# Residual merge and three later norms by halves of the tokens, with late modulation and softmax scaling moved

## The reference

```python
# layer 1
mod = silu(c) @ w_ada + b_ada                 # 6 vectors of 1024: sh1, sc1, g1, sh2, sc2, g2
h = rmsnorm(x) * (1 + sc1) + sh1
q, k, v, u_pool = split(h @ w_in)
att = softmax(rope(q) @ rope(k).T / 8) @ v    # 8 heads of 64, 2 kv heads, all 1024 keys
x = x + g1 * (concat(att, pool(u_pool)) @ w_out)
h2 = rmsnorm(x) * (1 + sc2) + sh2             # norm 1 of the kernel's count (q=1)
u = conv3(h2 @ w_up); gate, val = split(u)
x = x + g2 * ((silu(gate) * val) @ w_down)    # 2816 hidden channels
# layer 2
mod_l, mod_c = silu(c_2) @ w_ada_2 + b_ada_2, silu(c_ctx_2) @ w_ada_2 + b_ada_2
h = rmsnorm(x) * (1 + sc_l) + sh_l            # norm 2 (q=2)
# ... windowed attention with 256 context tokens, Fourier mix, gated convolution,
# three gated branches, one sum of 1024 channels ...
x = x + gt_l * (sums @ w_out_2)
out = rmsnorm(x)                              # norm 3 (q=3)
```

## Time and profile before

| | us |
|---|---|
| median of 3 runs | 2586.64 |
| lowest, highest | 2585.20, 2587.23 |
| the profiled execution | 2583.78 |
| its span in the trace | 2582.0 |
| PE busy | 2398.3 (93%) |
| DVE, ACT, POOL busy | 1098.6, 782.7, 794.9 |

### The profile page before, as it was taken

How to read it: one execution, slowest core, us unless ns; L and a number is a source line. 1 busy time by engine, 2 the same in 40 slices (tenths; PEclk the granted TensorE clock), 3 DMA queues, 4 the chain that set the end, 5 groups by cost and what they waited for, 6 DMA issues and landing times.

```text
span 2582.0 us, 31790 instructions
## 1 busy us (share of the span) xinstructions
PE 2398.3 (93%) x11742; PEld 2004.1 (78%) x11742; DVE 1098.6 (43%) x1333; ACT 782.7 (30%) x1077; POOL 794.9 (31%) x787
## 2 busy tenths in 40 slices
PE   4897999988999999999988989889999999999997
PEld 3586888766888888888777878778778888888885
DVE  7776888676441244123453341524221122222233
ACT  3226777303220122014414353444112111112210
POOL 1343222232333333323231331323223334333331
PEclk9898999998999999999998999999999999999998
DMA  5410000641111111111121101101001111111131
GB/s 226 172 44 34 17 16 25 257 175 33 49 49 49 49 49 48 42 65 49 37 94 70 62 27 51 53 16 72 28 25 49 49 49 54 50 46 41 49 122 73
DMA packets 45866, 165.46 MB, mean 64 GB/s; under 512 B 4208, under 2 KB 6000, under 8 KB 44656
## 3 DMA queue, kind: packets, MB, share of 16 engines
q1 hardware_dynamic: 45808, 164.67, 18.2%
HBM read 156.26 MB, written 8.39 MB: 64 GB/s over the span
## 4 chain that ended last, share of the span: by engine, by line
PE 75%; issue 10%; DVE 7%; POOL 3%; DMA 2%; ACT 2%; SPq 0%; DVEq 0%; POOLq 0%; ACTq 0%
PE acc L643 61%; PE bank L757 3%; PE turn L743 2%; PE acc L726 2%; DVE ADA L1328 2%; DMA ADA<-in_ada 2%; PE bank L743 1%; PE bank L881 1%; POOL EX L572 1%; POOL WH L497 1%; POOL WL L499 1%; PE bank L924 1%; DVE HL L1314 1%; PE bank L921 1%; DMA WF<-in_w 1%
## 5 line engine op out<-in xcount | busy, mean ns | idle before, releaser
L643 PE MATMUL acc<-HH,WH 128*128 128x512 f32 x1792 | 556.2, 392 | 7.3 <-POOL WL L499 6.7
L643 PE MATMUL acc<-HL,WH 128*128 128x512 f32 x1792 | 553.2, 390 | 0.0
L643 PE MATMUL acc<-HH,WL 128*128 128x512 f32 x1792 | 552.9, 390 | 0.0
L496 POOL TENSOR_TENSOR WH<-WF,CON 128x16 fp32r<-128x16 f32 x186 | 52.4, 282 | 1319.6 <-PE acc L643 1133.9
L499 POOL TENSOR_TENSOR WL<-WF,WH 128x1024 fp32r<-128x1024 f32 (+2 forms) x186 | 435.4, 2341 | 15.5
L643 PEld LDWEIGHTS acc<-HH,WH 128*128 128x128 f32 x1792 | 336.4, 188 | 80.5 <-POOL WL L499 6.1
L643 PEld LDWEIGHTS acc<-HL,WH 128*128 128x128 f32 x1792 | 337.5, 188 | 70.4
L643 PEld LDWEIGHTS acc<-HH,WL 128*128 128x128 f32 x1792 | 337.3, 188 | 70.3
L1586 DVE SCALAR_TENSOR_TENSOR CV<-EV,VEC,CV 128x1023 f32<-128x1023 f32 x44 | 106.1, 2410 | 245.5 <-ACT CV L1127 245.5
L497 POOL TENSOR_SCALAR WH<-WF 128x1008 fp32r<-128x1008 f32 (+2 forms) x186 | 187.3, 1007 | 0.0
L1527 DVE SCALAR_TENSOR_TENSOR XT<-acc,MOD,XT 128x1024 f32 (+1 forms) x40 | 51.2, 1282 | 247.3 <-PE acc L643 247.3
(11 more groups left out here) (303 smaller groups left out, 3757.1 us busy)
## 6 DMA issues: line engine op xcount, KB each, us to landing
WF<-in_w SPq DMA_DIRECT2D x150, 512.0 KB, 3.3
ADA<-in_ada SPq DMA_DIRECT2D x9, 2048.0 KB, 8.9
ADA<-in_ada SPq DMA_DIRECT2D x14, 1024.0 KB, 15.7
BIAS<-in_bias SPq DMA_DIRECT2D x8, 1152.0 KB, 5.2
XT<-in_xT SPq DMA_DIRECT2D x16, 512.0 KB, 9.7
WF<-in_w SPq DMA_DIRECT2D x24, 256.0 KB, 2.6
ADA<-in_ada SPq DMA_DIRECT2D x8, 512.0 KB, 3.3
out_xT<-XT SPq DMA_DIRECT2D x1, 4096.0 KB, 11.7
```

The lines of the kernel that those rows point to most:

```text
L496: pool.tensor_tensor(h[:, 0:FEW], f[:, 0:FEW], zero.to_broadcast([P, FEW]), ALU.add).then_inc(w_hi, 1)
L643: last = pe.matmul(acc[:, slot, HALF * c:HALF * c + HALF], w[slot][:, k, :], x[:, k, HALF * c:HALF * c + HALF], start=(k == 0 and w is WH ...
```

## The change

1. **Last residual tile by halves of the tokens** in norms 1, 2 and 3 (`gemm_by_halves`). PE does all chunks of tokens 0 to 511, then of 512 to 1023. After the first half DVE, ACT and PE do add, square, sum, stats, root, reciprocal and spread for these tokens, the PE parts between the chunks of the second half. The same is done for the second half once the tile is finished.
2. **The norm and the next two tiles by halves** (`normed_by_halves`, `modulate_by_halves`, `halves_pair`): all instructions on 512 tokens, twice as many. The stats and the spread of the second half stand inside PE's stream between chunks. `post_done` and the last `acc_read` are raised at the end of the norm's DVE work.
3. **Norm 3** multiplies and sends 16 blocks of 512 tokens.
4. **Modulation columns**: 16 of 36 stay in the residual tiles of `w_out` (four in each pair, one load ADA4 ahead of each); 20 move to the first four chunks of the first feed-forward group (`late_modulation`, five in each, four of them with a second pass), with their own loads ADA5 and condition vectors.
5. **Attention 1**: the maximum is one DVE instruction, which scales the scores in PSUM in place and takes their minimum as it goes; POOL multiplies the 128x1024 exponentials by the reciprocals (`normalise`) where it made the diagonal; PE turns them by transposes with the identity, 8 a unit.

```diff
-            def diagonal(it, u):
+            def normalise(it, u):
                 pool.wait_ge(rc_ready, it * 16 + (u + 1))
-                pool.tensor_tensor(DG[u % 2][:, :], ident, RC[:, u % 2:u % 2 + 1].to_broadcast([P, P]), ALU.mult
-                                   ).then_inc(dga_ready, 1)
+                x, r = EX[u % 4], RC[:, u % 2:u % 2 + 1]
+                pool.tensor_tensor(x[:, 0:FEW], x[:, 0:FEW], r.to_broadcast([P, FEW]), ALU.mult).then_inc(exn_ready, 1)
+                pool.tensor_scalar(x[:, FEW:], x[:, FEW:], r, 1.0, ALU.mult, ALU.mult).then_inc(exn_ready, 1)
...
-                            mm = pe.matmul(turns[q % 3][:, P * (k % 4):P * (k % 4) + P], EX[u % 4][:, P * k:P * k + P], DG[u % 2][:, :],
-                                           start=True, stop=True)
+                            mm = pe.transpose(turns[q % 3][:, P * (k % 4):P * (k % 4) + P], EX[u % 4][:, P * k:P * k + P], ident)
...
-                link(dve.tensor_reduce(MX[:, j:j + 1], acc[:, j, :], AX.X, ALU.max))
-                dve.tensor_tensor(NBI[:, j:j + 1], MX[:, j:j + 1], column(RSN, it * 16 + u), ALU.mult).then_inc(nb_ready, 1)
+                dve.tensor_scalar(acc[:, j, :], acc[:, j, :], column(RSN, it * 16 + u), None, ALU.mult, ALU.min,
+                                  accum_out=NBI[:, j:j + 1]).then_inc(nb_ready, 1)
...
+            def gemm_by_halves(n, slot, hi, lo, k_n, q):
+                pe.wait_ge(w_split, n + 1)
+                pe.wait_ge(acc_read, n - 1)
+                for h in range(2):
+                    for k in range(k_n):
+                        for w, x in ((WH, hi), (WH, lo), (WL, hi)):
+                            mm = pe.matmul(acc[:, slot, HALVES[h]], w[slot][:, k, :], x[:, k, HALVES[h]],
+                                           start=(k == 0 and w is WH and x is hi), stop=(k == k_n - 1 and w is WL))
+                        if k == k_n - 1:
+                            mm.then_inc(half_done if h == 0 else acc_done, 1)
+                        if h == 1 and k == 3:
+                            stats(q, SQS, 0)
+                        if h == 1 and k == 5:
+                            spread_rs(q, 0)
...
+            def halves_pair(n, q, context=None):
+                pe.wait_ge(w_split, n + 1)
+                pe.wait_ge(acc_read, n - 1)
+                if context is not None:
+                    context_gemm(context, 0)
...
+                def chunk(k, h, tiles):
+                    pe.wait_ge(hh_ready, chunk_base(q) + h * KD + k + 1)
+                    for s in tiles:
+                        products(k, s, h, WH, HH)
+                        products(k, s, h, WL, HH)
+                    pe.wait_ge(hl_ready, chunk_base(q) + h * KD + k + 1)
+                    for s in tiles:
+                        mm = products(k, s, h, WH, HL)
...
+                chunk(0, 0, (0,))
+                stats(q, SQS, 1)
+                chunk(1, 0, (0,))
+                pe.wait_ge(w_split, n + 2)
+                pe.wait_ge(half_added, 2 * q - 1)
+                chunk(0, 0, (1,))
+                chunk(1, 0, (1,))
+                chunk(2, 0, (0, 1))
+                chunk(3, 0, (0, 1))
+                spread_rs(q, 1)
+                for k in range(4, KD):
+                    chunk(k, 0, (0, 1))
+                pe.wait_ge(half_added, 2 * q)
+                for k in range(KD):
+                    chunk(k, 1, (0, 1))
...
+            def add_half(q, h, gate, stream):
+
+                x = stream[:, KD - 1, HALVES[h]]
+                dve.scalar_tensor_tensor(out=x, in0=acc[:, 1, HALVES[h]], scalar=gate(KD - 1), in1=x, op0=ALU.mult, op1=ALU.add
+                                         ).then_inc(half_added, 1)
+
+            def sum_half(q, h):
+                dve.wait_ge(half_squared, 2 * (q - 1) + h + 1)
+                dve.tensor_tensor(SQS[:, HALVES[h]], SQS[:, HALVES[h]], SQ[1][:, HALVES[h]], ALU.add).then_inc(sq_summed, 1)
+
+            def second_half_sums(q, n, gate, stream):
+                dve.wait_ge(acc_done, n + 1)
+                add_half(q, 1, gate, stream)
+
+            def normed_by_halves(q, n, gate, scale, shift):
...
+                def first(h, k):
+                    if k >= 3:
+                        dve.wait_ge(hl_ready, chunk_base(q) + h * KD + k - 2)
+                    dve.scalar_tensor_tensor(out=XN[k % 3][:, HALVES[h]], in0=XT[:, k, HALVES[h]], scalar=scale(k),
+                                             in1=turn[:, HALVES[h]], op0=ALU.mult, op1=ALU.mult).then_inc(xn_ready, 1)
+
+                def second(h, k):
+                    dve.wait_ge(hh_ready, chunk_base(q) + h * KD + k + 1)
+                    dve.scalar_tensor_tensor(out=HL[:, k, HALVES[h]], in0=XN[k % 3][:, HALVES[h]], scalar=shift(k),
+                                             in1=HH[:, k, HALVES[h]].bitcast(F32), op0=ALU.add, op1=ALU.subtract
+                                             ).then_inc(hl_ready, 1)
...
+                for h in range(2):
+                    dve.wait_ge(rb_done, norm_step(q, h))
+                    for k in range(KD):
+                        first(h, k)
+                        if h == 0 and k == 0:
+                            second_half_sums(q, n, gate, XT)
+                        if k > 0:
+                            second(h, k - 1)
+                        if h == 0 and k == 1:
+                            sum_half(q, 1)
+                        if h == 0 and k == 3:
+                            invert(q, 1)
+                    second(h, KD - 1)
+                dve.wait_ge(half_added, 2 * q)
+                dve.tensor_copy(MX[:, 2:3], eps).then_inc(acc_read, 1)
+                dve.tensor_copy(MX[:, 3:4], eps).then_inc(post_done, KD)
...
+                def last_pair():
...
+                    dve.scalar_tensor_tensor(out=x, in0=acc[:, 0, :], scalar=gate(KD - 2), in1=x, op0=ALU.mult, op1=ALU.add
+                                             ).then_inc(acc_read, 1)
+                    sum_squares(KD - 3, 1)
+                    sum_squares(KD - 2, 0)
+                    dve.wait_ge(sq_used, square_base(q) + KD - 1)
+                    if before_last:
+                        before_last()
+                    dve.wait_ge(half_done, q)
+                    add_half(q, 0, gate, stream)
+                    sum_half(q, 0)
+                    invert(q, 0)
...
-            for k in range(KD):
-                sp.wait_ge(out_ready, k + 1)
-                sp.dma_start(out[k], XT2[:, k, :]).then_inc(out_sent, 16)
-            sp.wait_ge(out_sent, 16 * KD)
+            for h, half in enumerate(HALVES):
+                for k in range(KD):
+                    sp.wait_ge(out_ready, h * KD + k + 1)
+                    sp.dma_start(out[k][:, half], XT2[:, k, half]).then_inc(out_sent, 16)
+            sp.wait_ge(out_sent, 32 * KD)
...
+            def late_modulation(c):
+
+                dve.wait_ge(ada5_in, 16 * (1, 3, 4, 5)[c])
+                for b in range(PER_CHUNK):
+                    i, w = ADA_FFN[PER_CHUNK * c + b], ADA5[:, b, :]
+                    if i < 48:
+                        modulation(w, C1D, MOD1[:, i:i + 1])
+                    else:
+                        modulation2(w, i - 48, C2D, JUNK)
...
+            dve.wait_ge(cond_ready, 7)
             for g, gk in enumerate(GROUPS):
-                gated_chunk(g, 0)
+                if g == 0:
+                    for c in range(4):
+                        late_modulation(c)
+                        gated_chunk(g, c)
+                    late_biases()
+                else:
+                    gated_chunk(g, 0)
...
+                if g == 0:
+
+                    sp.wait_ge(acc_done, N_OUT1 + KD)
+                    for v, c in enumerate((C1D, *C2D)):
+                        sp.dma_start(c[:, :], A["conds"][v]).then_inc(cond_in, 16)
+                    for c in range(4):
+                        if c > 0:
+                            for s in range(2):
+                                load_w(2 * c + N_UP[0] + s, s, "w8", 2 * c + w8 + s, KD)
+                            sp.wait_ge(ada_used, 52 + PER_CHUNK * c)
...
+                for h in range(2):
+                    for k in range(KD):
+                        act.wait_ge(xn_ready, chunk_base(q) + h * KD + k + 1)
+                        act.activation(HH[:, k, HALVES[h]], XN[k % 3][:, HALVES[h]], ACT.Identity, bias=shift(k)
+                                       ).then_inc(hh_ready, 1)
+                        if h == 0 and k == 0:
+                            square_half(q, 1, XT)
+                        if h == 0 and k == 2:
+                            root(q, 1)
```

## The result

The changed kernel takes 2552.88 us (median of 4 runs, 2551.84 to 2554.24) where the kernel before, beside it, takes 2585.97. The ratio is 0.9872, with a 95% interval of 0.9855 to 0.9889: 33 us faster, and not the 52 that were forecast. The time lies inside the range (2512 to 2565) but outside the forecast's own 2520 to 2550, at the foot of rival 1's times. The profiled executions differ by 2582.0 - 2552.3 = 29.7 us, and these are accounted for here.

What follows compares the result with a forecast made beforehand. PE was taken to bound the feed-forward layer and attention 1, with DVE next there, plus PE gaps elsewhere. Gains 30 + 12.2 + 6.9 - 4.6 + 7.4 = 51.9; 2583.8 - 51.9 + 2.9 = 2534.8 us, range 2512 to 2565.

Steps and rivals of the forecast that it cites:

- rival 1: Attention 1: in-place maximum dear or another loop link longer, such as late normalised exponentials; 2551 to 2573 us; chance 0.18.
- Attention 1: Attention stage of layer 1: two units fall from 7.81 to 6.9 us, gain 30 us, bounds 61 and a loss of 9.
- 0.2 is for ACT's copies of queries and outputs and the turn of the loop: Attention 1's loop: allowance of 0.2 us per two units, added to 6.7 to make 6.9.
- Rival 3: Attention 1: the clock falls and the kernel is slower than before, about 2675 us if all pairs run so; chance 0.05.
- Residual tiles: Tiles after attention 1: with 16 columns instead of 40 products DVE is never late; gain 12.2 us, bounds 9 and 12.5.
- Moved modulations: 24 products moved to the first feed-forward chunks, hidden by PE's tiles with some 1 us to spare; cost nothing.
- rival 2: First feed-forward chunks: the moved modulations do not fit and cost 10 us, giving 2545 us; chance 0.08.
- Norm 1: From the last residual tile's end to the first matmul after the pair: 42.5 us become 35.6, gain 6.9, bounds 4 and 10.
- Term (b): Norm 1, after the last tile's end: DVE's norm work, stats, spread and the pair's chunks take 27.5 us.
- Term (c): Norm 1, pair's end: POOL's split of the next weights takes 3.7 us plus up to 1.2 of blocking, 4.2 in all.
- Norm 2: Last tile to third tile's context: the later save delays weights, 47.0 us become 51.6, loss 4.6, bounds 0 and 7.
- The end: Norm 3 to the kernel's end: 24.1 us become 16.7 by half multiplications, gain 7.4 us, bounds 5 and 8.5.

Runs made afterwards that it cites:

- the last two kernels: All follow-up edits together on the changed kernel, 2523.39 us; and the same without its two edits of the late modulations, 2529.16 us.

## Why the prediction was right or wrong

**Attention 1, too high by 12 us.** The loop was sized right: its sum was 6.45 us for two units, and the intervals with neither gathering nor modulation are 6.49; those with the gathering were put at 6.9 and are 6.94 to 7.12. The average of 6.9 stands beside 6.81. PE waits for DVE's low parts before the values, as foretold, and does so in 22 places. (6.9 x 32 is 220.8, so the term's own gain was 29.1 us, and not 30.) The step that failed is "0.2 is for ACT's copies of queries and outputs and the turn of the loop". Three turns cost 3.3 us each above the other intervals, 9.7 above 6.9; some 4 us more lie at the two ends of the stage, which the product with 32 pairs did not hold; 2.5 come back because the other intervals are 6.81. The trace before had the turns: its intervals there are 9.35, not 7.48, and the average of 7.81 goes over them. The waits of PE in attention 1 by what was waited for (us in total, times, the longest), before and then after:

```profile
PE bank L743 <- POOL DG L527: 4.9, 3, 1.6
```

```profile
PE bank L848 <- DVE PTL L1648: 13.3, 22, 1.9
PE bank L835 <- POOL EX L561: 12.0, 7, 3.2
```

Three waits on POOL in a stage of four query blocks, one for each turn, was the line to have asked about. That the product on POOL "costs nothing", being asked for one unit later, was wrong at the turns, where it comes behind the gathering and 1.3 us of it lie open where 0.3 of the diagonal did. It also costs some 0.6 us in the intervals with a modulation column, where DVE's reciprocal is late.

**Rival 1 named the place** (normalised exponentials late behind other work on POOL), with ML in place of the query copies, and DVE's queue beside it. That the time lies at the foot of rival 1's is in part luck: its 12 us alone make 2547, inside the forecast's own range, and the rest comes from the norms. **Rival 3**, the clock, took part: after each of the three waits PE ran at half clock for 3 to 4 us, and the three intervals that follow are 1.2 us longer in sum. The transposes alone did not bring it: with the waits gone the clock is 0.99, in a stage in which transposes stand in every interval. The Trainium skill (TensorE: Matmul & The Clock Gate, PE-mode transpose) says that they do not count as busy time. By it one would look for a fall there; at this share, with 2.1 us of scores and 2.0 of values in 6.8, the measurement shows none.

**The transposes and the maximum.** Eight in 0.79 us (0.9 at most was forecast), the maximum 1.20 (1.2). Both nearest rows held.

**Residual tiles.** 12.4 for 12.2. The wait of 9.09 us is gone, and the one for the third tile's weights stays, as forecast:

```profile
483.92 0.72 PE L732 MATMUL acc<-MH,WH 128*128 128x512 f32 x2 [1.24 <-POOL WL L531]
```

**Moved modulations.** In the chunks they cost nothing, as forecast, and rival 2 did not come. The sum had DVE's time in it. It did not have SP's: with a tile 3.5 us earlier, weights came late. The slack of weights that are "asked for a tile later" was under 3.5 us.

**Norm 1, too high by 5.8 us.** In the tile 2.2 for 1.9. Term (b), the pair: 30.6 for 27.5. DVE's second sum came when forecast (5.1 us, not 5.0), but with PE's waits of 1.18 and 2.25 us half clock came into the pair, and lengthened it by 2.7 us; the sum had one clock term, of 2, behind the pair. There it was 2.4. Term (c), the split: "up to 1.2 of blocking", 4.2 in all; it was 6.1 of wait, since each of POOL's three instructions met one of DVE's. What the Trainium skill says of this port (SBUF — State Buffer, SBUF: two separate sides: an exclusive lock that is held for the whole instruction, against a DVE instruction with two SBUF inputs) agrees with the rows: 3.35 us for a product of 1.15.

**Norm 2, right in mechanism, short by 4.7 us.** The save behind the norm, the load behind the save, the split behind the load: each as told, each longer. In the tile 2.9 for 2.2; the save issued 25.3 us after the tile, not 23.4, since a half instruction on DVE takes 0.66 us start to start, not 0.6; the save 13.6, not 11.7; the split 5.2, not 3.7. From the pair's end to the context were 25 us, for "some 20". The price of the moved count was 15.4 us, as taking it back shows, not the 13 that the sum implies.

**The end.** 7.9 for 7.4.

## What to carry to other kernels

Before averaging a loop, list the intervals between one instruction's starts: what stands apart at the turn is a term of its own, and it is dear where an engine's queue has a step of the old turn ahead of the first step of the new one. When a count is raised later, look for every queue that waits on it: here one wait on a count of its own gave back 15 us. And a transfer that is hidden has a slack; a stage that is made faster ahead of it takes that slack first.

## What the runs showed of the hardware

- In the norms an instruction of DVE with two inputs starts every 0.66 us on 512 elements, where the whole ones before started every 1.19 to 1.20 on 1024: two halves cost a tenth more.
- Behind gaps of 5.7 to 6.3 us after norm 1's pair PE's first two matmuls took 1.21 or 1.22 us in all six traces with such a gap (half clock); behind 1.85 and 2.67 us they took 0.72 in three traces, full clock. Behind 3.6 us it went either way: 1.21, 0.81 or 0.72 for the same code. A start at half clock cost 2.4 us more in the changed kernel.
- The 4 MB save took 13.6 us when issued at the end of the norm, 11.7 before, and when made to wait for the last addition 11.7 by itself but 13.7 and 13.8 in the last two kernels, where weight loads of the third pair stand just ahead of it. No run shows what makes the 2 us.
